# Making the low parts of the v weights on GpSimd in place of VectorE, in the expert stage of a two-layer hybrid decoder

## What is computed

```python
q    = (xb @ wq)                                   # routing: top 16 of 128 x 128 keys, 8 heads
eidx, gate = top_k(...), softmax(...)              # 128 experts for each token
act  = gelu(einsum('td,tjd->tj', xb, u_tab[eidx]))
out  = einsum('tj,tjd->td', gate * act, v_tab[eidx])
```

## Time and profile before

| | us |
|---|---|
| median of three runs | 5458.6 |
| lowest and highest of them | 5452.01, 5473.6 |
| the profiled execution | 5468.3 (its span is 5466.5) |

### The profile page before, as it was taken

How to read it: one execution, slowest core, us unless ns; L and a number is a source line. 1 busy time by engine, 2 the same in 40 slices (tenths; PEclk the granted TensorE clock), 3 DMA queues, 4 the chain that set the end, 5 groups by cost and what they waited for, 6 DMA issues and landing times. The chain is left out here.

```text
span 5466.5 us, 79184 instructions
## 1 busy us (share of the span) xinstructions
PE 4238.1 (78%) x30618; PEld 3617.0 (66%) x30618; DVE 3373.7 (62%) x6218; ACT 1257.5 (23%) x1920; POOL 2034.7 (37%) x1116
## 2 busy tenths in 40 slices
PE   6965574905499999999988737567156999999998
PEld 6944564805498877877787627567145888778777
DVE  2164524789688888744422464438896788776444
ACT  2222212202232222222222231122022222222222
POOL 2200202236655587533131002022565455884331
PEclk9966777957799999999988768588578999999999
DMA  3120001102499999888521100020025999998885
GB/s 112 57 67 7 2 18 49 55 0 92 146 243 234 303 361 364 301 294 312 186 83 50 62 3 11 10 72 32 19 104 177 219 226 297 356 355 295 294 313 198
DMA packets 462790, 871.68 MB, mean 159 GB/s; under 512 B 224800, under 2 KB 280928, under 8 KB 458560
## 3 DMA queue, kind: packets, MB, share of 16 engines
q1 hardware_dynamic: 349888, 465.59, 27.8%
q0 software_dynamic: 112640, 402.71, 22.1%
HBM read 806.61 MB, written 61.58 MB: 159 GB/s over the span
## 5 line engine op out<-in xcount | busy, mean ns | idle before, releaser
L152 PE MATMUL ps<-x_split,w_split 128*128 128x384 f32 (+1 forms) x3104 | 1030.9, 332 | 143.1 <-DVE w_split L2134 92.8
L2077 PE MATMUL ps<-w_split,c_split 128*128 128x512 f32 x4608 | 1108.5, 394 | 0.8 <-DVE c_split L2152 0.8
L2077 PEld LDWEIGHTS ps<-w_split,c_split 128*128 128x128 f32 x4608 | 853.8, 188 | 277.0 <-issue 107.3
L154 PE MATMUL ps<-x_split,w_split 128*128 128x384 f32 (+1 forms) x3104 | 1010.4, 326 | 0.0
L153 PE MATMUL ps<-x_split,w_split 128*128 128x384 f32 (+1 forms) x3104 | 1009.7, 325 | 0.0
L152 PEld LDWEIGHTS ps<-x_split,w_split 128*128 128x128 f32 x3104 | 593.2, 191 | 268.3 <-issue 133.0
L2157 DVE CUSTOM_DVE_ANT_0 arena<-arena 64x1024 f32<-64x1024 f32 (+1 forms) x512 | 621.7, 1215 | 164.6 <-DMA arena<-pk_u_rows,arena 102.6
L153 PEld LDWEIGHTS ps<-x_split,w_split 128*128 128x128 f32 x3104 | 593.8, 191 | 4.0
L154 PEld LDWEIGHTS ps<-x_split,w_split 128*128 128x128 f32 x3104 | 592.9, 191 | 0.0
L2040 POOL DMA_INDIRECT arena<-pk_u_rows,arena x256 | 365.2, 1426 | 417.2 <-DVE arena L2157 381.8
L2009 ACT CAST w_split<-arena 128x1024 fp32r<-128x1024 f32 x256 | 268.6, 1049 | 1081.0 <-PE ps L2077 1080.1
(11 more groups left out here) (367 smaller groups left out, 6544.8 us busy)
## 6 DMA issues: line engine op xcount, KB each, us to landing
arena<-pk_u SPq DMA_DIRECT2D x256, 512.0 KB, 8.0
arena<-pk_v SPq DMA_DIRECT2D x256, 512.0 KB, 6.3
g_scratch<-arena SPq DMA_DIRECT2D x24, 2048.0 KB, 6.3
arena<-g_scratch SPq DMA_DIRECT2D x128, 384.0 KB, 8.0
arena<-w_in SPq DMA_DIRECT2D x28, 1024.0 KB, 5.4
arena<-pk_wq SPq DMA_DIRECT2D x16, 1024.0 KB, 6.4
arena<-cache_k SPq DMA_DIRECT2D x32, 256.0 KB, 2.7
arena<-cache_v SPq DMA_DIRECT2D x32, 256.0 KB, 3.5
```

Source lines behind the costliest of these rows:

```text
L152: pe.matmul(out, lhi, rhi, start=(n == 0), stop=False)
L154: last = pe.matmul(out, llo, rhi, start=False, stop=(n == len(terms) - 1))
L2077: done = pe.matmul(ps[:, 1 + 2 * j + n, :], c_of[hc], vs[:, s, hv, n * 512:(n + 1) * 512], start=first and m == 0, stop=last and m == 2, s ...
```

## The change

`v_lo` moves from VectorE's queue to GpSimd's. GpSimd does `v_lo(0)` after the fetches of block 0, and then in each round fetches for block b+1, makes `v_lo(b+1)` and fetches v rows for block b+2. The operation, its operands and its semaphores (`v_hi` is waited for, `v_ready` is raised) stay the same. VectorE's list loses one instruction in each block. Nothing else moves.

```diff
@@ GpSimd @@
+                    def v_lo(b, s):
+                        pool.wait_ge(v_hi, b + 1)
+                        pool.tensor_tensor(vs[:, s, 1], v_raw[:, s], vs[:, s, 0].bitcast(F32), ALU.subtract).then_inc(v_ready, 1)
+
                     fetch_u(0)
+                    v_lo(0, 0)
                     for b in range(BLOCKS):
                         fetch_u(b + 1)
+                        if b + 1 < BLOCKS:
+                            v_lo(b + 1, (b + 1) % 2)
                         fetch_v(b + 2)
@@ VectorE @@
-                    def v_lo(b, s):
-                        dve.wait_ge(v_hi, b + 1)
-                        dve.tensor_tensor(vs[:, s, 1], v_raw[:, s], vs[:, s, 0].bitcast(F32), ALU.subtract).then_inc(v_ready, 1)
-
...
                     u_lo(0, 0)
-                    v_lo(0, 0)
                     u_lo(1, 1)
...
                         if b and quad_at(b - 1) is not None:
                             summed(quad_at(b - 1), 1)
-                        if b + 1 < BLOCKS:
-                            v_lo(b + 1, (b + 1) % 2)
```

## The result

The changed kernel takes 5810.69 us (median, 5806.73 to 5828.48) against 5460.47 before: a ratio of **1.0642, with a 95% interval of 1.0619 to 1.0665**. The profiled execution's span is 5805.6 us, 339 us longer. The direction was forecast, the size was not: 350 us where 113 stood, above the range's upper end of 5690 us.

The account below looks back on a forecast made before the run. TensorE sets the pace, with VectorE's queue plus gather waits close behind early. Early 83, middle 30 and late 0 us make 113, which on a median of 5458.6 gives 5572 us; range 5480 to 5690.

Parts of the forecast that it names:

- What bounds the kernel before: Expert stage: TensorE sets the pace; early, VectorE with its gather waits comes next, 334.7 of 343 us; late, nobody.
- The port: Expert stage: GpSimd's 2.40 us subtraction blocks VectorE operations with two SBUF inputs, dots included; all 6.1 us a block exposed.
- v_lo on GpSimd would itself get longer: GpSimd in the expert stage: v_lo takes longer than 2.40 us, since it waits for VectorE in turn.
- rule that the second to start stands still: VectorE with two SBUF inputs against GpSimd reading SBUF: whichever instruction starts second blocks fully.
- The early sum: Early stretch, both layers: VectorE's path sets the pace at 9.6 and 9.95 us a block, 83 us lost together.
- TensorE's early waits are for u_lo: Early stretch: a sign that the forecast is right, TensorE waiting for VectorE's u_lo; no size given.
- still gets it in most blocks: TensorE gets v_lo in time in most blocks though v_ready comes later, since output(b) waits for product(b) as well.
- I price this at nothing: SyncE's queue: later v_ready delays loads of v and u and so ScalarE; priced at nothing, only widening the upper end.
- The middle sum: Middle stretch, both layers: a block takes 11.3 us, between VectorE's 10.7 and GpSimd's 12.6; 30 us lost.
- Rival (c): GpSimd bounds the middle stretch at 12.6 us a block, early as forecast: 194 us lost, 5653 us; chance 0.15.
- Rival (a): Dots don't contend, or v_lo slips under VectorE's waits and PSUM operations: 59 us gained, 5400 us; chance 0.10.
- The late stretch: Late stretch: no loss, since VectorE has half its time free and v_lo falls into its wait for the halves.

Follow-up runs that it names:

- idle_sub: Kernel before, v_lo kept on VectorE; GpSimd also makes an unused subtraction of the same form at v_lo's place in the changed kernel: 5555.6 us, ratio 1.0173.
- token_and_sub: Kernel before, v_lo kept on VectorE; GpSimd makes an unused subtraction, then raises v_ready, at v_lo's place in the changed kernel: 5786.2 us, ratio 1.0601.
- idle_memset: Kernel before, v_lo kept on VectorE; GpSimd also makes two 128x1024 memsets at v_lo's place in the changed kernel: 5472.0 us, ratio 1.0014.

## Why the prediction was right and wrong

**What bounds the kernel before**: right as far as the rows go. The early stretch had VectorE's list behind TensorE's, and the late one had room.

**The port**: right as a mechanism, and measured. The longest dot of layer 0 takes 4.03 us in the changed kernel. The forecast that v_lo on GpSimd would itself get longer came out in small part only (min/median/max):

```profile
L2160 DVE CUSTOM_DVE_ANT_0 arena<-arena x253: 1206/1210/4029, 1499.4 to 2453.6; 128x1024 f32<-128x1024 f32 x64, 64x1024 f32<-64x1024 f32 x63
```

```profile
L2056 POOL TENSOR_TENSOR w_split<-arena,w_split x118: 2346/2400/2717, 1505.1 to 2824.3; 128x1024 fp32r<-128x1024 f32 x118
```

GpSimd mostly keeps its 2.40 us, and VectorE pays for the collisions, even where its instruction starts first. The prediction's rule that the second to start stands still does not fit the starts in the trace. Two dots, each with the v_lo that starts 0.59 and 0.72 us behind it:

```profile
1625.34 4.03 DVE L2160 CUSTOM_DVE_ANT_0 arena<-arena 64x1024 f32<-64x1024 f32 x1 [0.59 <-DMA arena<-pk_u_rows,arena]
1625.93 2.35 POOL L2056 TENSOR_TENSOR w_split<-arena,w_split 128x1024 fp32r<-128x1024 f32 x1
...
1854.04 1.22 DVE L2160 CUSTOM_DVE_ANT_0 arena<-arena 64x1024 f32<-64x1024 f32 x1
1854.76 2.72 POOL L2056 TENSOR_TENSOR w_split<-arena,w_split 128x1024 fp32r<-128x1024 f32 x1
```

The first dot stands still and v_lo doesn't; the second runs on, and v_lo is 0.3 us longer. So it goes in both layers: of the VectorE instructions that start up to 0.62 us ahead of a v_lo and overlap it, all but three stand still until it is over, and the 29 that start 0.64 to 0.93 us ahead run on.

As a price the port alone, 95 us in `idle_sub`, is near the 113 us that the whole sum gave to it, but that is partly luck. In `idle_sub` VectorE keeps its 1.2 us of v_lo, so by the prediction's own sum an early block of layer 0 would take 7.3 + 2.4 + 1.0 + 0.1 = 10.8 us; it took 9.24. The port was priced too high, and the relief of VectorE, which showed no worth, was set against it. The earlier trace rows could also not show that an operation with an input in PSUM goes free, since that one ran after GpSimd's had ended; in the changed kernel the sums with such an input do (at most 0.69 us in layer 0).

**The early sum** was 83 us; it is 45 x (10.30 - 8.62) + 45 x (10.31 - 9.09) = 131 us. The path of 9.6 us a block left out the waits of the product for the gates, 84.5 us in this stretch of layer 0, and TensorE's own wait for v_lo, 48.1. The sign "TensorE's early waits are for u_lo" was wrong: they are 1.0 us there.

```profile
ACT w_split L2003 <- DMA arena<-pk_u: 98.4, 28, 7.8
...
DVE arena L2149 <- DMA arena<-g_scratch: 84.5, 21, 7.6
...
PE ps L2084 <- POOL w_split L2056: 48.1, 16, 7.7
```

That TensorE "still gets it in most blocks" held, but in 16 of some 42 it had to wait.

**The step that failed** is the sentence on SyncE's queue, "I price this at nothing". The prediction saw that `v_ready` comes later by most of a block and that SyncE waits for it in order. It named the load of u behind that wait, and gave ScalarE's wait for it as the sign, which did grow, from a nearly free 0.2 us of layer 0's early stretch to 98.4, and from 18.7 us in layer 1's to 69.6. But it did not follow the queue to its next entry, the load of the gates, once for two blocks, on which the product waits: 173.7 us in layer 0 where it had been 4.9. The kernel's text shows that entry, and the earlier trace rows show what a load of this queue takes to land. In place of nothing this step is worth most of the loss: issuing the gates ahead of the wait gives back 262 of 351 us (some 30 of them perhaps for another reason), and raising `v_ready` early 228.

**The middle sum** was 30 us; it is 31 x (13.68 - 10.62) + 31 x (13.74 - 10.98) = 180 us. It summed the busy time and the known waits of each engine by itself. The loss came from the ring shown above, whose length is no engine's sum: v_lo, the load of the gates (6.3 us in that block), the product with one step that stands still (2.6 us there), the sum, TensorE's wait and a half at the lower clock, and GpSimd's fetches. No step of the prediction asked what a wait of TensorE costs beyond its own length.

**Rival (c)** had GpSimd as the bound in the middle. It is busy 311 of 410 us. The gathers of `fetch_u` did shrink as argued, to a median of 938 ns from 1422.

**Rival (a)** needed dots that don't contend, and `idle_sub` shows that they do. Its gain was VectorE's relief, of which `token_and_sub` shows no worth here.

**The late stretch** was given nothing and lost 29 x (10.93 - 10.67) + 29 x (10.97 - 10.67) = 16 us. Its cover held but for 0.3 us a block, though not where the prediction had it: v_lo does not fall into VectorE's wait for the halves but on the product's first step, which takes 3.09 us there in the mean (2515 to 2820) where it took 0.56.

```profile
L2149 DVE TENSOR_TENSOR arena<-arena 128x384 f32<-128x384 f32 x28 | 86.6, 3093 | 82.5 <-ACT arena L2015 77.6 <-DMA arena<-g_scratch 4.9
```

The three sums make 327 us. From block 1 to block 127 the two layers together take 354 us more in the profiled executions; the rest of that lies mostly at the changes between the stretches, and all other stages together are 15 us shorter.

## What to carry to other kernels

When a step moves to another engine, first ask when its semaphore will be raised, and then read on, entry by entry, through every queue that waits for it in order: a load that has nothing to do with the step can stand behind it, as the gates did. Work that is moved behind gathers takes on their lateness, so it belongs ahead of them (228 of 351 us here) or its waiters must not hold others. Two small costs that meet in one ring can be worth much more than their sum, 328 us against 95 + 78 here, so a sum engine by engine can miss most of a loss.

## What the runs showed of the hardware

A VectorE CAST of 128x384, which has one SBUF operand, waits for GpSimd memsets (up to 2.38 us in place of 0.36) and for a GpSimd subtraction (2.93), while a dot with two operands waits for the subtraction (up to 4.03 us in place of 1.21) but not for the memset: its longest in `idle_memset` is 1.28 us.

```profile
L2168 DVE CUSTOM_DVE_ANT_0 arena<-arena x253: 1207/1217/1276, 1501.0 to 2279.6; 128x1024 f32<-128x1024 f32 x64, 64x1024 f32<-64x1024 f32 x63
```

A GpSimd subtraction of 128x1024 held up VectorE instructions that had started up to 0.62 us ahead of it; those that had started 0.64 us ahead or more ran on, and the subtraction took up to 2.79 us, once 3.69, in place of 2.40.

A pause of TensorE of 2.8 us was followed by a granted clock of 0.50, and cost about as much again as it lasted, 2.9 us on top of 2.9.
